# Out-projection and feed-forward as one stage: products in token order, first feed-forward weights in the scan state's place, pieces of 384, 512 and 256 tokens

## The reference, cut to what matters

```python
    x = x + gate_m * (jnp.concatenate([y_hy, y_ml], axis=-1) @ p['w_out'])
    h = _rmsnorm(x, p['norm_ffn_w']) * (1 + scale_f) + shift_f
    up = (h @ p['ffn_w_up']).reshape(B, rows, L // rows, 2 * D_FF)
    up = _dwconv2d(up, p['ffn_conv_w'], p['ffn_conv_b']).reshape(B, L, 2 * D_FF)
    a, val = jnp.split(up, 2, axis=-1)
    x = x + gate_f * ((jax.nn.silu(a) * val) @ p['ffn_w_down'])
```

## Time and profile before

| what | us |
|---|---|
| median of 3 runs | 1685.43 |
| lowest, highest | 1684.05, 1687.31 |
| the profiled execution's own time | 1686.27 |
| its span in the trace | 1684.4 |
| TensorE busy | 1569.1 (93%) |
| VectorE busy | 1010.3 (60%) |
| ScalarE, GpSimd busy | 478.8, 461.3 |

### The profile page before, as it was taken

One profiled execution on the slowest core, in us unless ns is written; L12 is line 12 of the kernel. 1 busy time (PEld: TensorE's weight loads), 2 busy tenths in 40 slices (PEclk: granted clock), 3 DMA queues, 4 the chain that ended last, 5 costly groups with the idle time before them and its releaser, 6 DMA issues.

```text
span 1684.4 us, 22849 instructions
## 1 busy us (share of the span) xinstructions
PE 1569.1 (93%) x9581; PEld 1451.4 (86%) x9581; DVE 1010.3 (60%) x1396; ACT 478.8 (28%) x672; POOL 461.3 (27%) x194
## 2 busy tenths in 40 slices
PE   4697999999999969899879999999999999999997
PEld 1396789988899969799869999999999999999996
DVE  5768233866533426611788837863884588288846
ACT  1553122232333347541522211220220121122203
POOL 1525121422211149124322312221322223223210
PEclk8788999999999989999989999999999999999998
DMA  8563313353354597510011101111101101101102
GB/s 330 188 251 150 157 58 124 119 187 122 108 171 141 203 285 232 176 50 1 26 50 51 50 26 51 38 38 50 50 26 51 42 34 51 51 25 51 34 30 113
DMA packets 110570, 168.11 MB, mean 100 GB/s; under 512 B 5755, under 2 KB 87811, under 8 KB 105347
## 3 DMA queue, kind: packets, MB, share of 16 engines
q1 hardware_dynamic: 109039, 164.24, 28.6%
q10 hardware_dynamic: 1428, 2.40, 0.4%
HBM read 135.35 MB, written 31.27 MB: 99 GB/s over the span
## 4 chain that ended last, share of the span: by engine, by line
PE 49%; DVE 2%; ACT 1%; POOL 0%; issue 0%; DVEq 0%
PE psum L231 16%; PE psum L233 16%; PE psum L235 16%; DVE mlp_acc_a L2985 1%; POOL ffn_h_lo L2878 0%; PE psum L3181 0%; DVE w_raw L3039 0%; DVE w_raw L3087 0%; ACT w_raw L2931 0%; DVE ffn_h_lo L3049 0%; ACT ffn_h_hi L2935 0%; DVE mlp_acc_a L3039 0%; DVE mlp_acc_a L3087 0%; DVE tail_x L3009 0%; PE psum L3131 0%
## 5 line engine op out<-in xcount | busy, mean ns | idle before, releaser
L231 PE MATMUL psum<-ffn_h_hi,w_hi 128*128 128x320 f32 (+2 forms) x1104 | 267.3, 341 | 12.8 <-DVE mlp_acc_a L2985 11.4
L2985 DVE SCALAR_TENSOR_TENSOR w_raw<-psum,par,w_raw 128x945 f32<-128x945 f32 (+2 forms) x176 | 214.7, 1220 | 93.0 <-ACT w_raw L2906 89.3
L233 PE MATMUL psum<-ffn_h_lo,w_hi 128*128 128x320 f32 (+2 forms) x1104 | 265.6, 339 | 0.0
L235 PE MATMUL psum<-ffn_h_hi,w_lo 128*128 128x320 f32 (+2 forms) x1104 | 265.5, 339 | 0.0
L2985 DVE SCALAR_TENSOR_TENSOR mlp_acc_a<-psum,par,mlp_acc_a 128x945 f32<-128x945 f32 (+2 forms) x176 | 214.5, 1219 | 37.2 <-ACT mlp_acc_a L2906 34.1
L2824 POOL TENSOR_TENSOR w_lo<-w_raw,w_hi 128x2048 fp32r<-128x2048 f32 x32 | 147.8, 4620 | 287.9 <-ACT w_hi L2818 287.9
L231 PEld LDWEIGHTS psum<-ffn_h_hi,w_hi 128*128 128x128 f32 x1104 | 181.2, 188 | 30.9 <-issue 11.6
L233 PEld LDWEIGHTS psum<-ffn_h_lo,w_hi 128*128 128x128 f32 x1104 | 181.3, 189 | 16.4
L235 PEld LDWEIGHTS psum<-ffn_h_hi,w_lo 128*128 128x128 f32 x1104 | 181.1, 188 | 16.4
L3009 DVE SCALAR_TENSOR_TENSOR tail_x<-psum,mod,tail_x 128x384 f32<-128x384 f32 (+1 forms) x192 | 94.8, 515 | 128.2 <-PE psum L235 128.0
L233 PE MATMUL psum<-mlp_g_lo,w_hi 128*128 128x384 f32 x480 | 161.3, 336 | 0.0
(11 more groups left out here) (362 smaller groups left out, 2677.1 us busy)
## 6 DMA issues: line engine op xcount, KB each, us to landing
w_raw<-ffn_w_up SPq DMA_DIRECT2D x22, 1024.0 KB, 5.1
filt_ada<-ada_w SPq DMA_DIRECT2D x16, 1024.0 KB, 7.8
w_raw<-w_in SPq DMA_DIRECT2D x13, 1024.0 KB, 5.5
w_raw<-ffn_w_down SPq DMA_DIRECT2D x11, 1024.0 KB, 5.1
scan_rows_spread<-scratch_scan_rows SPq DMA_DIRECT2D x18, 512.0 KB, 6.1
rownorm_ada<-ada_w SPq DMA_DIRECT2D x8, 1024.0 KB, 7.8
rownorm_x<-x_sample SPq DMA_DIRECT2D x8, 512.0 KB, 8.3
scratch_kt<-kt_spec SPq DMA_DIRECT2D x4, 1024.0 KB, 4.4
```

What stands on the lines that cost most here:

```text
L231: ins = nc.tensor.matmul(out, wh, x_hi(k, i), start=begin, stop=False)
L233: ins = nc.tensor.matmul(out, wh, x_lo(k, i), start=False, stop=False)
L235: ins = nc.tensor.matmul(out, wl, x_hi(k, i), start=False, stop=end)
L2985: ins = stt(out=out, in0=image(up_at)[:, r0 + dy:r1 + dy, c0 + dx:c1 + dx], scalar=weight(i, loc, t), in1=out, op0=ALU.mult, op1=ALU.add)
```

## The change

`mixer_output` and `feed_forward` become one function and one block, `output_and_feed_forward`. There is no barrier between them, and the semaphores of both are cleared in one row at the end.

- Out-projection products 0 to 3 stay as they were. Products 4 to 7 are cut into 12, each of one token range and one output block, in the order of `SHARED`: range 0 (384 tokens) for blocks 4 to 7, then range 1 (512), then range 2 (256), in PSUM banks 0 to 4 in turn. Bank 5 takes the token sums. Sums, root, diagonals and spread of a range are placed between later ranges' products.
- The feed-forward's ranges are now 384, 512 and 256 tokens instead of 320, 512 and 320, from `LEAD` 128 instead of 192.
- The 24 chunks have 6 places instead of 3. In the first two ranges GpSimd makes every second low part. VectorE makes the low part of a chunk 3 chunks later instead of 2.
- The first feed-forward weights' high and low part go to the memory of `g_lo` (which lies where the scan state and its spare were), so the ring isn't needed for them.
- Step 0's products 0 and 1 go range by range: (0,0), (0,1), (1,0), (0,2), (1,1), (1,2), the first number being the product, the second the range. So product 0 ends two ranges before product 1.
- `y_hi` and `y_lo` are the tensors `h_hi` and `h_lo`, aligned to 64 bytes. In the scan, three small tensors move into spare memory and the keys lie in the order in which chunks are first read.

The core of the diff (of the tables only what sets ranges, places and splitters; the orders of the engines are shown as rows below):

```diff
+PIECES_OUT = ((0, 384), (384, 896), (896, T))
+SHARED = tuple((p, n) for p in range(3) for n in range(4, 8))
+SHARED_BANK = (0, 1, 2, 3, 4, 0, 1, 2, 3, 4, 1, 2)
+WHOLE = 4
...
-    LEAD = 192
-    PIECES = ((0, 320), (320, 832), (832, T))
+    LEAD = 128
+    PIECES = PIECES_OUT
...
+        h_hi = ph.sb("h_hi", [P, KD, T], F32R, align=64)
+        h_lo = ph.sb("h_lo", [P, KD, T], F32R, align=64)
+        y_hi, y_lo = h_hi, h_lo
...
-        places = [acc_a[:, 1, 0:512], acc_a[:, 1, 512:1024], mem["w_raw"][:, 1, 1152:1664]]
+        places = [acc_a[:, 1, 0:512], acc_a[:, 1, 512:1024]] + [mem["w_raw"][:, 1, 512 * i:512 * i + 512] for i in range(4)]
+        first_hi, first_lo = (g_lo[:].rearrange("p j t -> p (j t)")[:, UNIT * i:UNIT * i + UNIT] for i in range(2))
...
         def splitter(n):
+            if n < 2 * KD:
+                return "pool" if n % 2 else "dve"
             return "pool" if n % 3 == 2 else "dve"
...
+            def shared_square(m):
+                p, n = SHARED[m]
+                act.wait_ge(x_added, WHOLE + m + 1)
+                act.wait_ge(squares_added, WHOLE + m)
+                nc.scalar.activation(square[:, tokens_of(p)], x[:, n, tokens_of(p)], ACT.Square).then_inc(squared, 1)
...
+            def shared_product(m):
+                p, n = SHARED[m]
+                ring.ready(pe, n // 2)
+                bank, tok = SHARED_BANK[m], tokens_of(p)
+                before = [i for i in range(m) if SHARED_BANK[i] == bank]
+                pe.wait_ge(x_added, WHOLE + before[-1] + 1 if before else 3 if bank < 3 else 4)
...
+            for m in range(len(SHARED)):
+                if m == 5:
+                    token_sums(0)
+                if m == 6:
+                    spread(0)
+                if m == 9:
+                    token_sums(1)
+                if m == 10:
+                    spread(1)
+                shared_product(m)
+            first_product(0, 0, range(KD))
+            token_sums(2)
+            first_product(0, 1, range(3))
+            spread(2)
+            first_product(0, 1, range(3, KD))
+            first_product(1, 0, range(KD))
+            first_product(0, 2, range(KD))
+            first_product(1, 1, range(KD))
+            first_product(1, 2, range(KD))
```

More of the change, by code:

```diff
@@ L266, in __exit__, with sb @@
         return self.ctx.__exit__(*a)
[L268 to L269 removed]
+    def sb(self, name, shape, dt=F32, side="left", align=32):
+        return self.ctx.enter_context(self.nc.sbuf_tensor(f"{self.name}_{name}", shape, dt, side=side, align_bytes=align))
     def sem(self, name):
@@ L1982, in chunk_units, with chunk_scan @@
     return units
[L1985 to L1998, removed]
+CSIZE = 2 * 8 * (HD + 1)
+def chunk_scan(nc, io, mem, dram, x, hacc, C, spare, sum_sq, parts_in, last_out):
     ps = mem["psum"]
@@ new lines, in chunks @@
+            def chunks(ns, flush=False):
+                for n in ns:
+                    scale_chunk(n)
+                    if n % KD >= LAG or n >= 2 * KD:
+                        split_chunk_lo(n - LAG)
+                if flush:
+                    for n in range(ns[-1] + 1 - LAG, ns[-1] + 1):
+                        split_chunk_lo(n)
+            nc.vector.tensor_scalar(ss[:], ss[:], 1.0 / HD, EPS, ALU.mult, ALU.add).then_inc(mean, 1)
+            hyena_lo(0)
+            dve.wait_ge(root_ml, 1)
@@ new lines, in _ @@
+            step.do(nc.vector.reciprocal(ss[:], ss[:]))
+            gate_chunk(0)
+            hyena_lo(1)
+            gate_chunk(1)
+            hyena_lo(2)
+            gate_chunk(2)
+            mlstm_lo(0)
+            hyena_lo(3)
+            for t in range(3, NT):
+                gate_chunk(t)
+                mlstm_lo(t - 2)
+            mlstm_lo(NT - 2)
+            mlstm_lo(NT - 1)
+            dve.wait_ge(x_done, 2 * NT)
+            for n in range(WHOLE):
+                dve.wait_ge(full, n + 1)
+                add_gated(nc, slot_banks(ps, n), x[:, n, :], mem["mod"][:, 16 + n, :]).then_inc(x_added, 1)
@@ new lines, in _ @@
+            for m in range(5):
+                add_shared(m)
+            token_stats(0)
+            token_scales(0)
+            add_shared(5)
+            chunks(range(4))
+            add_shared(6)
+            chunks(range(4, KD), flush=True)
+            for m in range(7, 9):
+                add_shared(m)
+            token_stats(1)
+            token_scales(1)
+            add_shared(9)
+            chunks(range(KD, KD + 2))
+            add_shared(10)
+            chunks(range(KD + 2, KD + 4))
@@ new lines, in out_weights, with block @@
+            def out_weights(n):
+                wh, wl = cols(ring.hi(n // 2), 256), cols(ring.lo(n // 2), 256)
+                c = (n % 2) * P
+                return (lambda k: wh[:, k, c:c + P]), (lambda k: wl[:, k, c:c + P])
+            def block(n, chunks):
+                slot = slot_banks(ps, n)
+                ins = product(nc, [slot[:, i, 0:BW] for i in range(NB)], *out_weights(n), lambda k, i: y_hi[:, k, third(i)],
+                              lambda k, i: y_lo[:, k, third(i)], chunks, first=chunks[0] == 0, last=chunks[-1] == KD - 1)
+                if chunks[-1] == KD - 1:
+                    ins.then_inc(full, 1)
```

723 lines of the change are left out of this document (374 added, 349 removed).

## The result

| | before | after | ratio, 95% interval |
|---|---|---|---|
| median of the first comparison, us | 1686.37 (4 runs) | 1675.51 (4 runs, 1669.87 to 1676.56) | 0.9930 (0.9904 to 0.9956) |
| the same two kernels, second comparison, us | 1688.68 (11 runs) | 1671.74 (6 runs, 1668.95 to 1675.78) | 0.9908 (0.9889 to 0.9928) |
| span of the profiled executions, us | 1684.4; 1684.4 | 1673.0; 1667.5 | |

I forecast 1670.7 us (1664 to 1677), 14.7 less than before. Measured: 10.9 less by the medians, then 16.9 less; by the ratios 11.8 and 15.5 us less, with intervals that overlap. The first median lies inside the range and 4.8 us above the forecast, the second 1.0 us above it. So the sum was right in size. Its terms were not, and the rest of this text is about them.

What follows compares the result with a forecast made beforehand. TensorE was taken to bound the kernel, by its matmuls, the seam and what follows the last store: -14.2 + 0.3 - 3.7 + 2.9 = -14.7 us, giving a forecast median of 1670.7 us (range 1664 to 1677).

Steps and rivals of the forecast that it cites:

- The seam: Between out-projection and feed-forward: TensorE restarts with product 2 at 837.8 instead of 852.0 us, a gain of 14.2 us.
- the walk: TensorE's new order followed from 754.3 us, with 1.6 us of waits, to product 0's end at 826.0 us.
- The named waits: At the seam: TensorE waits for range 1's sum (0.3 to 0.7 us) and its low parts (0.7 to 1.2 us).
- The clock: Behind the seam's remaining wait: 3.4 us at half speed lose 1.7 us, today's 1.4 go; net +0.3 us.
- The ranges of the feed-forward: New split in 1008 trios of the feed-forward: 3.7 ns less each, -3.7 us; bounds -10.1 us and 0.
- The sum of the single widths: Feed-forward trio price from adding its three matmuls, 173 + 230 + 119.5 = 522.5 ns; not the price taken.
- rival 1: Feed-forward: the new split of a trio has no effect, 530 ns stay; 1674.4 us, chance 0.17.
- What I had at nothing: Costed at zero: block's end between the stages, moved scan tensors, six places, later loads, final norm and stores.
- The end: After the last store: 41 more semaphore clearings on GpSimd at 71 ns each, +2.9 us.

Runs made afterwards that it cites:

- e5: The changed kernel run again without edits; ratio 0.9908 to the kernel before.
- e3: The changed kernel with 14 unread 512-column matmuls filling TensorE's wait before product 2 of step 0; ratio 0.9902 to the kernel before.
- e1: The kernel before with only the feed-forward split changed to 384, 512, 256 columns; 1681.83 us, ratio 0.9966.
- e2: The changed kernel with the old split (320, 512, 320) in steps 1 to 10; ratio 0.9907 to the kernel before.
- e7: The changed kernel with its two tensors of normalised tokens 32 bytes further on; ratio 0.9909 to the kernel before.
- e11: The changed kernel with four places for chunks instead of six; one execution, 156.3 us from TensorE's restart after the scan to product 2 of step 0.
- e6: The changed kernel with products 0 and 1 of step 0 side by side, as in the kernel before; ratio 0.9926 to the kernel before.
- e10: The changed kernel with i unread 64-column matmuls ahead of each step i from 1 to 10; one execution, span 1676.8 us.
- e8: The changed kernel with 14 unread matmuls in the wait and 40 semaphores cleared in step 3; 1665.66 us, ratio 0.9876 to the kernel before.

## Why the prediction came out as it did

**The seam: right mechanism, 2.3 us too favourable.** From the end of whole product 3 to the end of product 0 the walk gave 71.7 us. In e5 it is 73.5: 50.5 for the range-wise products (50.2 in the walk), 3.7 for sums and spreads (3.2), 17.4 for step 0 without its waits (16.7), 1.9 of waits (1.6). The named waits were right; what I missed is that each break of TensorE's stream also makes its neighbours longer. Behind one, the first matmul of 512 columns stands for 312 to 340 ns instead of 233, as here behind the second wait (timeline of TensorE, after, the first two matmuls and one gap of 233), and a product near a break runs at 235 to 237.

```profile
821.98 0.50 PE L231 MATMUL psum<-mlp_h_hi,tail_g_lo 128*128 128x512 f32 x1 [1.02 <-DVE mlp_h_lo L2967]
822.32 0.39 PE L233 MATMUL psum<-mlp_h_lo,tail_g_lo 128*128 128x512 f32 x1
822.55 0.40 PE L235 MATMUL psum<-mlp_h_hi,tail_g_lo 128*128 128x512 f32 x1
```

The convolution took 12.0 us from product 0's end and not 11.8, and 0.3 us stand before the end of whole product 3. The idle time before mark 2 was 3.5 us (3.4 predicted). The rest of the first execution's loss is the whole products at 530 ns, 0.5 us, and the ranges of 384 columns at 177 instead of 173 ns.

**The clock: right, between the forecast and the bound.** The half clock behind the wait was 6.8 us in the first execution and 3.4 in the second. The filling shows that the idle time causes it and that it is worth about 2 us (e3). Forecast: 1.7 lost; bound: twice that.

**The ranges of the feed-forward: right sign, wrong price and wrong owner.** I took 3.7 us, with 10.1 as the bound. The trios average 521.3 ns, so 8.8 us came, more than double the term. I had reasoned that a row of nearly the same shape is the best price (526.3 ns), and that the price belongs to the shape. The sum of the single widths (522.5), which I set aside, is within 1 ns of what e1 shows. In the profiles the price goes with the program and, within the changed one, with the moment:

| split of a trio | in the kernel before | in the changed kernel |
|---|---|---|
| 320, 512, 320 | 530 (two executions) | 523.4 (e2) |
| 384, 512, 256 | 523.4 (e1) | 520, in stretches 526.7 |
| 384, 384, 384, out-projection | 520 (two executions, and e1) | 520, 524 or 530 |

e1 and e2 have one profile each, so that their 523.4 ns would stand in a second execution is not shown by traces; their times, over 12 and 6 runs, agree with it. What the change did beside the split to take 2 to 7 ns off both is open. It is not the start of the rows by 32 bytes (e7), nor the four or six places (e11), nor the order of the first products (e6). I didn't try the new places of the other tensors.

By the gap of N/2.4 + 2.5 ns that the Trainium skill's page "TensorE: Matmul & The Clock Gate", section "Back-to-back issue gap", gives for an isolated warm matmul, the split would have been worth nothing. That was rival 1, and e1 refutes it, by 5.7 us.

**What I had at nothing: 2 us.** The eight to ten late starts of 0.22 us are in no term of mine. They come at the same places in the changed kernel and its variants, 100 and 50 us apart in turn, shorter in e1 and e2 (some 0.06 us), and all but one go when instructions are put in (e10). The kernel before has none in two executions. Their cause is open.

**The end: right.** 74 clearings, 71 ns each; moved away, 2.3 of the 2.8 us come back.

So from mark 2 to the end I had -0.5 us: +0.3, -3.7, +2.9. It is about -3: trios -8.8, late starts +2.0, clearings +2.9, clock +0.3 to +1.7. And of the -14.7 in all, -14.9 came by the marks (11.9 and about 3). Two errors of 2.3 and 2.5 us cancelled, by luck.

**The rest between executions.** Mark 1 stood anywhere from 681.0 to 688.8 us in eleven profiles of the changed kernel and its variants, although TensorE's work ahead of it is the same. The granted clock there shows why in part: of the changed kernel's two executions the first has 0.93, the second 0.94 from 20 to 680 us.

```profile
20.00:680.00 660.00, 596.08 (x3987) 537.67 (x3986) 363.34 (x548) 235.41 (x403) 208.23 (x114) 0.93 0.50 174
```

```profile
20.00:680.00 660.00, 592.92 (x4003) 534.28 (x4001) 361.33 (x561) 237.87 (x414) 209.62 (x114) 0.94 0.51 175
```

The two spans differ by 5.5 us, and 3.6 of them stand ahead of mark 1. That the gains of 10.9 and 16.9 us differ for the same reason is likely and not shown: only one execution of each comparison was profiled. The kernel before varies as much in its time (1683.69 to 1692.28 us in the second comparison). Its three profiles have mark 1 at 683.0 to 683.8 us, the eleven at 684.7 on average, so whether the tensors that the change moved in the scan cost the front anything is not told.

## What to carry to other kernels

Measure an edit of a long kernel from marks in the trace that stand around it, since here the unchanged front alone moved by 7.8 us between executions. A wait that can't be removed can be filled with unread matmuls, and semaphores can be cleared where their engine idles. When two kernels differ in the price of the same matmul, don't give it to the edit that seems to explain it before you have undone that edit in the one and made it in the other.

## What the runs showed of the hardware that I had not expected

- The same stream of matmuls runs at one of several fixed prices. A trio of three 384s took 520 or 530 ns in two executions of the same program (524 in e8 and e10, which are the same up to there), and kept its price for over 100 matmuls. 384, 512, 256 took 520 or 526.7, and changed at a late start or behind a break.
- A matmul of 64 columns with its own weights costs 112 ns start to start (each more in e10), where one of 256 costs 113.6 (22 in 2.50 us from 836.01 us). The Trainium skill, "TensorE: Matmul & The Clock Gate", section "LDWEIGHTS (loading the stationary operand)", gives P/1.2 ns, 106.7 for a load of 128 columns. By that rule the load would be the floor, and the trace agrees to 5 ns at 64 columns; that it is the load that sets the floor, no run here shows.
- After 3.5 us of idle time the half clock held for 6.8 us in one execution and for 3.4 us in the other of the same program.
